# Modulation of an attention and expert block: two thirds summed on VectorE, two gates moved, table loads moved

## Chip, cores and metric

One core of a Trainium2 chip. The metric is the device time of one execution in microseconds (us). Before the change the median of three runs is 3347.15 us.

## What is computed

One layer over 1024 tokens of width 1024, in float32. Cut to what matters here:

```python
mod = silu(c) @ w_ada + b_ada                       # w_ada: 1024 x 6144
shift1, scale1, gate1, shift2, scale2, gate2 = split(mod, 6)
h = rmsnorm(x, g1) * (1 + scale1) + shift1
qa, ka, va, qb, kb, vb, ga, gb = split(h @ w_in)
y_sb = stick_breaking_attention(qa, ka, va)          # 8 heads, strictly causal
y_sw = sliding_window_sink_attention(qb, kb, vb)     # 8 heads, softmax with a sink
x = x + gate1 * ((sigmoid(ga) * (y_sb @ sb_proj) + sigmoid(gb) * (y_sw @ sw_proj)) @ w_out)
h2 = rmsnorm(x, g2) * (1 + scale2) + shift2
# per token 8 heads x top 16 of 16384 experts; expert rows of u and v are gathered
x = x + gate2 * sum(softmax(score) * gelu(h2 . u[e]) * v[e])
out = rmsnorm(x, gf)
```

## The kernel before

The 1024 tokens are eight blocks of 128, in groups of 2, 3 and 3 blocks. Each group goes through the mixer: normalisation and transposes (H), values (V), for each of four pairs of heads the q/k product (QK) and the stick-breaking scores (SB), the window projections (SWP) and window attention (SW), the merge of both branches with gates (MG), the output projection (OUT), and the queries and keys of the expert layer (PREP). Beside the mixer of later groups runs the expert stream: for each block 128 tiles. GpSimd gathers a tile of 128 expert rows of 8 KB (`uv`, line 651) into one of ten ring slots, VectorE takes dot products (line 1597), ScalarE GELU and a diagonal of weights (lines 1270, 1276), TensorE adds up (line 1036), and that frees the slots. No gather can start before the first queries and keys of block 0 are done.

**Order.** Each engine's program is a set of Python generators merged by `interleave`: each yields a key and the smallest key goes next. The order is fixed when the kernel is built, and every engine executes its own list strictly in order, waits included. The keys come from `Plan`, called as `at(stage, group, item, later)`; `later` is added to the key. For group 0 the plan puts H at -208.35, V at -201.14 and -197.45, QK of the four pairs at -192.77, -182.08, -171.40 and -160.72, the first SB step of a pair 4.2 and the second 6.05 behind its QK, SWP at -150.03, SW at -135.40 and MG at -118.66. SyncE issues all transfers but the gathers and five small constants, in one queue.

**Modulation.** `w_ada` is read as 12 column groups of 512, in three thirds of four (`r` = 0, 1, 2), 8.4 MB each. A third fills `wada`, 16384 floats per partition at the start of the ring, in four transfers: two halves of the contraction times two pairs of column groups. TensorE multiplies with `cb`, silu(c) spread over 32 columns: 8 steps `k` times 4 column groups, each group on its own 32 columns of the array, into bank `VACC`. A float32 matmul counts as two instructions in the trace. VectorE adds the bias into `md` and forms 1 + scale times gain. Row 0 (shift 1 and scale 1) is needed for h; rows 1 and 2 (gates, shift 2 and scale 2) are written to `mods_dram` and read back for OUT. In TensorE's order third 1 stands ahead of pair 0, third 2 ahead of pair 1. `wada` is free for the next third when the matmuls of the last one are done (`ada_mm`). The window weights of group 0 go to `RINGO + 1024 * a`, which is inside `wada`.

**Pairs.** The values are stored to `v_dram` (v_scratch in the trace, line 484) and read back per pair (line 500); TensorE waits for that read (`in_vp`) before a pair's scores (line 850). The q/k product of a pair is line 837. For group 0 a pair has two steps, each with logs on ScalarE, a softplus on VectorE (line 1451), sums (lines 865, 870) and values (line 879) on TensorE. The keys of a pair are stored to `k_dram` (line 507); the next pair's ScalarE copy waits for that.

**Window and merge.** In SW, TensorE makes the scores of a block (line 949), the softmax runs on VectorE and ScalarE, TensorE transposes (line 964) and multiplies with the values (line 976). In MG, each of eight column groups has two gate products (`q` = 0, 1; line 731), and two projections (line 734). ScalarE's `Tables.use` issues a table load (line 106) where the next function is in another table than the last.

## Time and profile before

| | |
|---|---|
| median of three runs | 3347.15 us (3343.45 to 3355.85) |
| profiled execution | 3351.51 us, span from first to last instruction 3349.7 us |
| TensorE busy | 2180.0 us (65%) |
| VectorE busy | 2033.7 us (61%) |
| ScalarE busy | 1149.4 us (34%) |
| GpSimd busy | 1113.3 us (33%) |
| moved by DMA | 1267.98 MB, mean 379 GB/s; gathers 1074.03 MB |
| mean granted TensorE clock | 0.798 of full |

The shares are means over a run whose beginning differs from the rest, so they say little about a change in the beginning. The page also cuts the span into 40 slices; read there how busy the DMA engines are, slice by slice. The trace's times are from the start of the span.

### The profile page before, as it was taken

Reading aid. Unit: us, or ns where it says so; the run is one execution under the profiler, and the core shown is the slowest. Engines: PE = TensorE matmul, PEld = TensorE weight load, DVE = VectorE, ACT = ScalarE, POOL = GpSimd, SP = SyncE. Lnnn points to the kernel's source line nnn. Section 1 sums busy time; section 2 is a strip of 40 time slices with the busy share of each in tenths; the row PEclk is TensorE's granted clock in tenths of the full one; section 3 lists DMA queues with packets and bytes.
Section 4 is the critical chain, followed back from the end, with each engine's and each line's share of the span. In section 5 each row is a group of like instructions: output and inputs, shape, how many; then the busy total and the mean of one; then the engine's idle time right before and its main releaser. Section 6 shows DMA issues by size and latency. Waiting matters only on the chain.

```text
span 3349.7 us, 35574 instructions
## 1 busy us (share of the span) xinstructions
PE 2180.0 (65%) x11116; PEld 980.9 (29%) x11116; DVE 2033.7 (61%) x4779; ACT 1149.4 (34%) x3644; POOL 1113.3 (33%) x1033
## 2 busy tenths in 40 slices
PE   5878768877987776777775888577433443344333
PEld 2566633343533332323333333233100000010000
DVE  1022457776656566777667666756666666666754
ACT  1210246733223233676634222222322232222221
POOL 0000124332433333433343333343444444434442
PEclk8989989888998888888897998788765665666565
DMA  9524789989999999999999999999999999999997
GB/s 355 203 87 149 288 345 358 396 360 355 408 416 416 420 406 416 376 415 403 394 408 368 420 419 418 397 417 420 417 421 415 419 408 421 418 416 403 422 421 328
DMA packets 198911, 1267.98 MB, mean 379 GB/s; under 512 B 21609, under 2 KB 35977, under 8 KB 54977
## 3 DMA queue, kind: packets, MB, share of 16 engines
q0 software_dynamic: 147616, 1074.03, 77.9%
q1 hardware_dynamic: 51104, 191.67, 14.9%
q8 instruction: 88, 1.44, 0.2%
q14 instruction: 103, 0.84, 0.1%
HBM read 1244.36 MB, written 21.25 MB: 378 GB/s over the span
## 4 chain that ended last, share of the span: by engine, by line
DMA 38%; PE 35%; issue 10%; ACT 9%; DVE 4%; POOL 1%; SPq 1%; another core or an unknown queue 0%; POOLq 0%; DVEq 0%; ACTq 0%
DMA arena<-in_uv,idx_r 30%; PE pb L1036 12%; PE pb L731 5%; PE pb L816 4%; ACT dg L1276 3%; PE pb L734 2%; DMA arena<-in_w_ada 2%; PE pb L751 2%; DMA arena<-in_w_q 2%; ACT L106 2%; PE pb L1022 2%; PE pb L837 1%; POOL arena L651 1%; DMA v_scratch<-arena 1%; DVE arena L1597 1%
## 5 line engine op out<-in xcount | busy, mean ns | idle before, releaser
L651 POOL DMA_INDIRECT arena<-in_uv,idx_r x1024 | 1110.2, 1084 | 2208.1 <-PE pb L1036 1597.0
L1597 DVE CUSTOM_DVE_ANT_0 arena<-arena 128x1024 f32<-128x1024 f32 x1024 | 1251.6, 1223 | 774.7 <-DMA arena<-in_uv,idx_r 730.9
L1036 PE MATMUL pb<-arena,dg 128*32 128x512 f32 x4096 | 726.1, 845 | 814.6 <-ACT dg L1276 761.2
L1036 PEld LDWEIGHTS pb<-arena,dg 128*32 128x32 f32 x4096 | 132.8, 136 | 1280.2 <-ACT dg L1276 930.1
L1270 ACT ACTIVATE gl<-dots 128x4 f32<-128x4 f32 x256 | 52.9, 207 | 1015.0 <-DVE dots L1597 1002.2
L816 PE MATMUL pb<-arena 128*128 128x384 f32 (+1 forms) x768 | 254.2, 486 | 27.7 <-issue 19.8
L106 ACT ACT_TABLE_LOAD x171 | 219.4, 1283 | 107.9 <-DVE dots L1597 58.8
L1276 ACT ACTIVATE dg<-ig,gl 128x32 f32<-128x32 f32 x1024 | 246.6, 312 | 8.5 <-ACT gl L1270 0.3
L1265 ACT ACTIVATE ig<-istack,gate_r 128x32 f32<-128x32 f32 x1024 | 243.3, 311 | 0.0
L731 PE MATMUL pb<-arena 128*128 128x384 f32 (+1 forms) x768 | 235.4, 459 | 2.4 <-ACT arena L1123 2.4
L816 PEld LDWEIGHTS pb<-arena 128*128 128x128 f32 x768 | 152.2, 205 | 136.5 <-issue 78.5
L731 PEld LDWEIGHTS pb<-arena 128*128 128x128 f32 x768 | 143.6, 191 | 95.8 <-issue 29.1
L751 PE MATMUL pb<-arena 128*128 128x512 f32 x256 | 118.8, 621 | 15.7 <-DVE arena L1438 8.5
L837 PE MATMUL pb<-arena 128*128 128x384 f32 (+1 forms) x384 | 117.8, 460 | 0.0
L734 PE MATMUL pb<-arena 128*128 128x384 f32 (+1 forms) x384 | 117.4, 457 | 0.0
L1451 DVE SCALAR_TENSOR_TENSOR arena<-pb,arena 128x384 f32<-128x384 f32 (+2 forms) x120 | 51.6, 471 | 105.3 <-ACT arena L1205 103.6
L865 PE MATMUL pb<-arena,tri 128*128 128x384 f32 (+2 forms) x240 | 93.2, 482 | 15.4 <-DVE arena L1451 13.8
L1254 ACT ACTIVATE arena<-pb 128x256 f32<-128x256 f32 x112 | 42.9, 383 | 168.1 <-PE pb L1022 156.5
L1022 PE MATMUL pb<-arena,ident 128*32 128x256 f32 x896 | 78.5, 425 | 27.5 <-ACT arena L1254 20.8
L879 PE MATMUL pb<-arena 128*64 128x384 f32 (+2 forms) x240 | 65.1, 491 | 38.4 <-ACT arena L1213 34.4
L837 PEld LDWEIGHTS pb<-arena 128*128 128x128 f32 x384 | 71.7, 192 | 49.7 <-issue 18.3
L850 PE MATMUL pb<-arena 64*128 64x384 f32 (+2 forms) x240 | 57.1, 558 | 43.7 <-DMA arena<-k_scratch 32.0
(157 smaller groups left out, 2217.7 us busy)
## 6 DMA issues: line engine op xcount, KB each, us to landing
arena<-in_w_ada SPq DMA_DIRECT2D x12, 2048.0 KB, 17.8
arena<-in_w_mg SPq DMA_DIRECT2D x24, 1024.0 KB, 5.0
arena<-in_w_q SPq DMA_DIRECT2D x24, 1024.0 KB
arena<-in_uv,idx_r POOLq DMA_INDIRECT x1024
arena<-in_w_qk SPq DMA_DIRECT2D x12, 1024.0 KB, 16.3
arena<-in_w_mg SPq DMA_DIRECT2D x24, 512.0 KB, 5.9
arena<-in_x SPq DMA_DIRECT2D x16, 512.0 KB, 16.4
arena<-in_w_out SPq DMA_DIRECT2D x4, 2048.0 KB, 12.0
```

Source lines behind the costliest of these rows:

```text
L106: self.act.add_instruction(mybir.InstLoadActFuncSet(name=self.nc.get_next_instruction_name(), act_func_set_id=table, engine=mybir.EngineTy ...
L651: pool.indirect_dma_start(ring[:, i % RING, :], None, uv, bass.IndirectOffsetOnAxis(ap=idx_r[:, b % 2, 4 * n + c:4 * n + c + 1], axis=0)). ...
L731: m = pe.matmul(bank, gates[:, q * KT + k, :], hT[:, k, 0:T], start=(k == 0), stop=(k == KT - 1))
L734: m = pe.matmul(bank, projections[:, (q - 2) * 4 + k, :], y[:, k, 0:T], start=(k == 0), stop=(k == 3))
L751: m = pe.matmul(pb[:, BGB + 2 * (j % 2) + i, :], merged[:, k, j * P:(j + 1) * P], f(out_home(g, k) + i * HALF, HALF), start=(k == 0), stop ...
L816: m = pe.matmul(pb[:, BGB + p, 0:T], wq[:, p * KT + k, :], h2T[:, k, 0:T], start=(k == 0), stop=(k == KT - 1))
L837: m = pe.matmul(pb[:, BGB + i, 0:T], wqk[:, i * KT + k, :], hT[:, k, 0:T], start=(k == 0), stop=(k == KT - 1))
L1022: x_ = pe.matmul(pb[32 * q:32 * q + 32, MISC, 256:512], selector(c), h2cur[:, 256 * i:256 * i + 256], start=True, stop=True)
L1036: m = pe.matmul(pb[32 * c:32 * c + 32, VACC + i, :], dg[:, STEP * n // 4 % 2, c, :], ring[:, (STEP * g + c - first) % RING, D + i * HALF:D ...
L1265: op = act.activation(ig[:, half, first + c], istack[:], ACT.Copy, scale=gate_r[:, b % 2, STEP * n + c:STEP * n + c + 1])
L1276: op = act.activation(dg[:, half, first + c], ig[:, half, first + c], ACT.Copy, scale=gl[:, a + c:a + c + 1])
L1597: dve.tensor_tensor_reduce(u, h2rep[:, slot(b, c), :], u, 1.0, 0.0, ALU.mult, ALU.add, dots[:, i % 8:i % 8 + 1]).then_inc(dots_done, 1)
```

## The change

- Third 0 is loaded in quarters of the contraction (two steps `k`, all four column groups), ahead of the biases and gains; TensorE waits quarter by quarter.
- Thirds 1 and 2 are loaded in quarters too, but VectorE sums them: 16 instructions a third, over 2 column groups of 512, each multiplying the weights with silu(c) of its partition and adding to `wsum`. TensorE then adds over partitions with four matmuls of `negones`, and VectorE subtracts the result from the bias. A quarter of third 2 is loaded when the four sums that read its place are done.
- TensorE's product of third 1 now stands ahead of pair 1, that of third 2 ahead of SWP.
- The window weights of group 0 move out of `wada`; these, the table of distances (`alibi`), the merge and the output weights are issued at other places of SyncE's order.
- The two gate products of the first column group of MG in group 0 are made inside SW, into the two accumulator banks.
- In eight places a table load is issued ahead of the semaphore wait and not behind it.

```diff
@@ -251,6 +251,7 @@
         wada = rows(RINGO, 4, 4096)
+        wsum = [rows(YF + 2048 * r, 4, HALF) for r in range(2)]
         md = rows(MD, 3, HALF)
@@ -288,7 +289,9 @@
-            return RINGO + 1024 * a if g == 0 else (X0, X0 + 1024, W0 + 2048, W0 + 6144, B0 + 1536, W0)[a]
+            if g == 0:
+                return (X0, X0 + 1024, RINGO + 18432, W0 + 6144, RINGO + 16384, RINGO + 17408)[a]
+            return (X0, X0 + 1024, W0 + 2048, W0 + 6144, B0 + 1536, W0)[a]
@@ -376,36 +379,40 @@
                     sp.dma_start(small[:, 0:KT], c8).then_inc(in_c, 16)
+                    ada(0, 0)
+                    ada(0, 1)
+                    for j in range(SIZE[0]):
+                        sp.dma_start(xt[:, j, :], x[j * P:(j + 1) * P, :]).then_inc(in_x[j], 16)
+                    ada(0, 2)
+                    ada(0, 3)
                     for c in range(4):
...
                         sp.dma_start(gg[32 * c:32 * c + 32, :], g[(c % 2) * HALF:(c % 2 + 1) * HALF].partition_broadcast(32)).then_inc(in_g, 16)
-                    for k in range(2):
-                        for c in range(2):
-                            ada(0, k, c)
-                        if k == 0:
-                            for j in range(SIZE[0]):
-                                sp.dma_start(xt[:, j, :], x[j * P:(j + 1) * P, :]).then_inc(in_x[j], 16)
                     for i in range(2):
                         value_weights(i)
-                    for p in range(3):
+                    sp.dma_start(f(qk_home(0, 0), 2048), w_qk[0]).then_inc(in_wqk[0], 16)
+
+                def ada(r, i):
+                    sp.dma_start(wada[:, :, 1024 * i:1024 * (i + 1)],
+                                 w_ada[4 * r:4 * r + 4, :, 2 * i:2 * i + 2, :].rearrange("c p k n -> p c (k n)")).then_inc(in_ada[i], 16)
+
+                def mods():
+                    yield at("H", 0, 0, 1)
+                    sp.wait_ge(ada_mm, 1)
+                    for i in range(4):
+                        ada(1, i)
+                    for p in range(1, 3):
                         sp.dma_start(f(qk_home(0, p), 2048), w_qk[p]).then_inc(in_wqk[p], 16)
                     sp.dma_start(sink_row[:], sinks.partition_broadcast(P)).then_inc(in_sink, 16)
-
-                def ada(r, k, c):
-                    sp.dma_start(wada[:, 2 * c:2 * c + 2, 2048 * k:2048 * (k + 1)],
-                                 w_ada[4 * r + 2 * c:4 * r + 2 * c + 2, :, 4 * k:4 * (k + 1), :].rearrange("c p k n -> p c (k n)")).then_inc(in_ada[2 * k + c], 16)
-
-                def mods():
+                    for i in range(4):
+                        yield at("QK", 0, 0, i)
+                        sp.wait_ge(ada_sums, 4 * (i + 1))
+                        ada(2, i)
                     for r in range(1, 3):
-                        yield at("H", 0, 0, 1) if r == 1 else at("QK", 0, 0, 0.6)
-                        sp.wait_ge(ada_mm, r)
-                        for k in range(2):
-                            for c in range(2):
-                                ada(r, k, c)
-                        yield at("QK", 0, r - 1, 0.5)
+                        yield at("QK", 0, 1, 0.5) if r == 1 else at("SWP", 0, 0, 1)
                         sp.wait_ge(md_done, r + 1)
@@ -418,24 +425,29 @@
                     sp.dma_start(f(qk_home(0, 3), 2048), w_qk[3]).then_inc(in_wqk[3], 16)
-                    yield at("QK", 0, 2, -1)
+                    window_weights(0, 3, 1)
+                    yield at("QK", 0, 1, 0.2)
+                    sp.wait_ge(qk_mm, 2)
+                    window_weights(0, 0, 2)
+                    yield at("QK", 0, 2, 0.2)
+                    sp.wait_ge(qk_mm, 4)
+                    window_weights(0, 4, 1)
+                    window_weights(0, 5, 1)
+                    yield at("QK", 0, 3, 0.2)
+                    sp.wait_ge(qk_mm, 6)
+                    window_weights(0, 2, 1)
+                    yield at("SWP", 0, 0, 0.5)
                     sp.wait_ge(ada_mm, 3)
-                    window_weights(0, 0, 2)
-                    window_weights(0, 3, 1)
-                    window_weights(0, 4, 1)
-                    window_weights(0, 2, 1)
-                    window_weights(0, 5, 1)
-                    sp.wait_ge(qk_mm, 2)
-                    sp.dma_start(alibi, consts[:, 2 * P + TOPK + 32:2 * P + TOPK + 32 + TABLE]).then_inc(in_alibi, 16)
                     merge_weights(0, 0)
                     merge_weights(0, 1)
-                    yield at("QK", 0, 3)
-                    sp.wait_ge(qk_mm, 6)
                     out_weights(0, 0, 4)
-                    out_weights(0, 4, 4)
+                    yield at("SWP", 0, 2, 1)
+                    sp.wait_ge(sw_mm, 2)
+                    sp.dma_start(alibi, consts[:, 2 * P + TOPK + 32:2 * P + TOPK + 32 + TABLE]).then_inc(in_alibi, 16)
                     yield at("SW", 0, 0)
...
                     merge_weights(0, 2)
+                    out_weights(0, 4, 4)
                     for ft in range(3, KT):
@@ -655,18 +667,20 @@
                     for r in range(3):
-                        yield at("H", 0, 0, -2) if r == 0 else at("QK", 0, r - 1, -0.01)
+                        yield at("H", 0, 0, -2) if r == 0 else at("QK", 0, 1, -0.01) if r == 1 else at("SWP", 0, 0, -0.01)
                         if r == 0:
                             pe.wait_ge(c_wide, 1)
+                            for k in range(KT):
+                                if k % 2 == 0:
+                                    pe.wait_ge(in_ada[k // 2], 16)
+                                for c in range(4):
+                                    m = pe.matmul(pb[32 * c:32 * c + 32, VACC, :], cb[:, k, :], wada[:, c, k * HALF:(k + 1) * HALF],
+                                                  start=(k == 0), stop=(k == KT - 1))
                         else:
+                            pe.wait_ge(ada_sums, 16 * r)
                             pe.wait_ge(md_done, r)
-                        for k in range(KT):
-                            if k % 4 == 0:
-                                pe.wait_ge(in_ada[k // 2], 16 * (r + 1))
-                                pe.wait_ge(in_ada[k // 2 + 1], 16 * (r + 1))
                             for c in range(4):
-                                m = pe.matmul(pb[32 * c:32 * c + 32, VACC, :], cb[:, k, :], wada[:, c, k * HALF:(k + 1) * HALF],
-                                              start=(k == 0), stop=(k == KT - 1))
+                                m = pe.matmul(pb[32 * c:32 * c + 32, VACC, :], negones[:, 0:32], wsum[r - 1][:, c, :], start=True, stop=True)
                         m.then_inc(ada_mm, 1)
@@ -715,9 +729,10 @@
                             pe.wait_ge(ysw_done, FIRST[g + 1])
-                        pe.wait_ge(in_wmg[mg_turn(g, ft)[0]], mg_turn(g, ft)[1])
+                        if n:
+                            pe.wait_ge(in_wmg[mg_turn(g, ft)[0]], mg_turn(g, ft)[1])
                         gates, projections = rows(mg_home(g, ft)[0], 2 * KT, P), rows(mg_home(g, ft)[1], KT, P)
-                        for q in range(4):
+                        for q in range(2 if n == 0 else 0, 4):
                             o = 4 * ft + q
@@ -897,6 +912,16 @@
                     values(len(steps) - 1)
+
+                def first_gate(q):
+
+                    if q == 0:
+                        pe.wait_ge(in_wmg[mg_turn(0, 0)[0]], mg_turn(0, 0)[1])
+                        pe.wait_ge(md_done, 3)
+                    gates = rows(mg_home(0, 0)[0], 2 * KT, P)
+                    for k in range(KT):
+                        m = pe.matmul(pb[:, VACC + q, 0:SIZE[0] * P], gates[:, q * KT + k, :], hT[:, k, 0:SIZE[0] * P], start=(k == 0), stop=(k == KT - 1))
+                    m.then_inc(mg_mm, 1)
@@ -983,6 +1008,8 @@
                             scores(j + 1)
+                        if g == 0:
+                            first_gate(j)
                         yield at("SW", g, j, 5)
@@ -1046,8 +1073,8 @@
                     yield -2000
+                    table.use(GELU)
                     act.wait_ge(in_c, 16)
-                    table.use(GELU)
                     act.activation(small[:, 8:16], small[:, 0:8], ACT.Tanh, scale=0.5).then_inc(c_tanh, 1)
@@ -1100,8 +1127,8 @@
                         off = CHUNK if b == 0 else 0
+                        table.use(EXP_LN)
                         act.wait_ge(peaked, b + 1)
-                        table.use(EXP_LN)
                         for h in range(SW_HEADS):
@@ -1129,20 +1156,20 @@
                             yield at("MG", g, ft, part(g, 3.8 + 3.7 * q))
+                            if table.now == EXP_LN or table.now == SQRT:
+                                table.use(GELU)
                             act.wait_ge(mg_mm, 4 * n + q + 1)
...
                                 act.wait_ge(mg_done, n - 1)
-                            if table.now == EXP_LN or table.now == SQRT:
-                                table.use(GELU)
-                            act.activation(sg[:, 2 * (ft % 2) + q, 0:T], pb[:, AVB + (4 * ft + q) % 5, 0:T], ACT.Tanh, scale=0.5).then_inc(mg_th, 1)
+                            act.activation(sg[:, 2 * (ft % 2) + q, 0:T], pb[:, VACC + q if n == 0 else AVB + (4 * ft + q) % 5, 0:T], ACT.Tanh, scale=0.5).then_inc(mg_th, 1)
                     for j in range(GB):
...
                         yield at("OUT", g, j, 12.5)
+                        table.use(SQRT)
                         act.wait_ge(o_rinv, b + 1)
-                        table.use(SQRT)
                         act.activation(stats[:, 40 + j:41 + j], stats[:, 36 + j:37 + j], ACT.Sqrt).then_inc(o_rstd, 1)
@@ -1229,8 +1256,8 @@
                             yield topk_at(b, m) + topk_span(b, m) - 1
+                            table.use(EXP_LN)
                             act.wait_ge(picked, n + 1)
-                            table.use(EXP_LN)
                             act.activation(best[:], best[:], ACT.Exp).then_inc(picked_exp, 1)
@@ -1265,8 +1292,8 @@
                             yield STEP * (g + 1) + 0.5
+                            table.use(GELU)
                             act.wait_ge(dots_done, STEP * (g + 1))
-                            table.use(GELU)
                             act.activation(gl[:, a:a + STEP], dots[:, a:a + STEP], ACT.Gelu).then_inc(gelu_done, 1)
@@ -1282,8 +1309,8 @@
                         yield TILES * (b + 1) + 11.5
+                        table.use(SQRT)
                         act.wait_ge(fin_rinv, b + 1)
-                        table.use(SQRT)
                         act.activation(stats[:, 50:51], stats[:, 49:50], ACT.Sqrt).then_inc(fin_rstd, 1)
@@ -1306,12 +1333,27 @@
                     for r in range(3):
-                        yield at("H", 0, 0, -1.5) if r == 0 else at("QK", 0, r - 1, 0.1)
+                        if r:
+                            for n in range(16):
+                                yield at("V", 0, 0, 2 + 0.9 * n) if r == 1 else at("QK", 0, 1 + n // 6, 0.2 + 1.1 * (n % 6))
+                                k, c = n // 2, 2 * (n % 2)
+                                if n % 4 == 0:
+                                    dve.wait_ge(in_ada[n // 4], 16 * (r + 1))
+                                w, total = wada[:, c:c + 2, k * HALF:(k + 1) * HALF], wsum[r - 1][:, c:c + 2, :]
+                                if k == 0:
+                                    dve.tensor_scalar(total, w, cb[:, k, 0:1], None, ALU.mult).then_inc(ada_sums, 1)
+                                else:
+                                    dve.wait_ge(ada_sums, 16 * (r - 1) + n - 1)
+                                    dve.scalar_tensor_tensor(out=total, in0=w, scalar=cb[:, k, 0:1], in1=total, op0=ALU.mult, op1=ALU.add).then_inc(ada_sums, 1)
+                        yield at("H", 0, 0, -1.5) if r == 0 else at("QK", 0, 1, 0.1) if r == 1 else at("SWP", 0, 0, 0.2)
                         if r == 0:
...
                         dve.wait_ge(ada_mm, r + 1)
-                        link(dve.tensor_tensor(md[:, r, :], pb[:, VACC, :], brow[:, r, :], ALU.add))
+                        if r:
+                            link(dve.tensor_tensor(md[:, r, :], brow[:, r, :], pb[:, VACC, :], ALU.subtract))
+                        else:
+                            link(dve.tensor_tensor(md[:, r, :], pb[:, VACC, :], brow[:, r, :], ALU.add))
                         if r == 0:
```

## Rows read from the trace of the kernel before

**Rows 1.** Busy time, granted clock, DMA share and GB/s of two stretches of the whole run.
```profile
150.00:200.00 50.00, 33.42 (x191) 28.56 (x192) 14.03 (x29) 10.98 (x44) 0.00 (x0) 0.78 0.10 37
...
900.00:1200.00 300.00, 235.97 (x1032) 108.67 (x1020) 175.54 (x393) 83.55 (x273) 105.90 (x96) 0.87 1.01 418
```

**Rows 2.** Chain of waits in the first 120 us: start, length, what.
```profile
7.39 24.29 DMA arena<-in_w_ada
...
31.82 5.28 PE pb L668 x32
...
38.57 26.77 DMA arena<-in_w_ada
...
74.70 22.19 DMA arena<-in_w_ada
...
118.38 12.03 DMA arena<-v_scratch
```

**Rows 3.** Timeline of TensorE and SyncE: start, length, engine, line, operation, idle before.
```profile
42.83 16.91 PE L706 MATMUL pb<-arena 128*128 128x512 f32 x32 [3.43 <-DVE arena L1338]
...
69.20 0.34 SPq L500 DMA_DIRECT2D arena<-v_scratch  x1
...
70.73 7.17 PE L837 MATMUL pb<-arena 128*128 128x256 f32 x32
...
78.38 0.49 PE L850 MATMUL pb<-arena 64*128 64x128 f32 x4 [0.47 <-ACT arena L1182]
...
87.56 3.64 PE L668 MATMUL pb<-arena,cb 128*32 128x512 f32 x32
...
102.02 7.17 PE L837 MATMUL pb<-arena 128*128 128x256 f32 x32
...
138.25 7.17 PE L837 MATMUL pb<-arena 128*128 128x256 f32 x32
...
152.97 14.08 PE L914 MATMUL pb<-arena 128*128 128x256 f32 x64
```

**Rows 4.** Fine windows of the DMA engines: 2 KB, 8 KB and 4 KB rows, and the queue running dry.
```profile
5.00:6.00 1.00, 0.00 (x0) 0.00 (x0) 0.00 (x0) 0.00 (x0) 0.00 (x0) 1.00 1.06 231
...
12.00:14.00 2.00, 0.00 (x0) 0.00 (x0) 0.00 (x0) 0.00 (x0) 0.00 (x0) 1.00 1.02 426
...
21.50:22.00 0.50, 0.50 (x8) 0.14 (x4) 0.00 (x0) 0.38 (x3) 0.00 (x0) 1.00 1.05 442
...
67.00:68.00 1.00, 1.00 (x12) 0.36 (x7) 0.00 (x0) 0.00 (x0) 0.00 (x0) 0.50 0.25 81
```

**Rows 5.** VectorE: the three-operand instruction by form, and one softplus in the timeline.
```profile
L1434 DVE SCALAR_TENSOR_TENSOR arena<-arena,stats 128x1024 f32<-128x1024 f32 x2 | 2.6, 1284 | 1.8 <-ACT stats L1146 1.8
...
82.38 0.76 DVE L1451 SCALAR_TENSOR_TENSOR arena<-pb,arena 128x256 f32<-128x256 f32 x2 [0.90 <-ACT arena L1205]
```

**Rows 6.** Timeline of TensorE from the window softmax to the merge.
```profile
178.25 2.77 PE L949 MATMUL pb<-arena 64*128 64x192 f32 x16 [2.53 <-DVE arena L1370]
...
187.49 1.97 PE L964 MATMUL pb<-ident,arena 128*128 128x128 f32 x8 [6.48 <-DVE arena L1387]
...
198.53 3.67 PE L964 MATMUL pb<-ident,arena 128*128 128x128 f32 x16 [6.53 <-DVE arena L1387]
...
205.69 7.17 PE L731 MATMUL pb<-arena 128*128 128x256 f32 x32 [0.69 <-ACT arena L1123]
...
317.47 1.04 PE L744 MATMUL pb<-ident,arena 128*128 128x128 f32 x8
```

**Rows 7.** Timeline of GpSimd: the first gather.
```profile
377.95 1.00 POOL L651 DMA_INDIRECT arena<-in_uv,idx_r  x1 [373.78 <-ACT idx_r L1240]
```

**Rows 8.** Table loads: all of them, their longest cause of idle, and one in the timeline.
```profile
L106 ACT ACT_TABLE_LOAD  x171: 1283/1283/1283, 2.4 to 3343.8; - x171
...
  DVE dots L1597: 58.8, 25
...
371.61 1.28 ACT L106 ACT_TABLE_LOAD   x1
```

4 lines of the change are left out of this document (2 added, 2 removed).

## The prediction

> **What bounds the kernel now.** I read first the page's line of DMA share over forty slices and then two coarse windows [rows 1]. In the window from 900 to 1200 us the DMA engines are busy all the time (share 1.01, 418 GB/s): the gathers of expert rows, 1,074 of 1,268 MB, flow from the first gather to the end of the run. In the window from 150 to 200 us they are nearly idle (share 0.10). The first gather is issued at 377.95 us [rows 7], because it needs the first queries of group 0, and these need the whole mixer of group 0. So the run is an opening of 378 us, and then a stream whose length is bytes over bandwidth. A microsecond taken out of the opening should come off the end nearly whole; one taken out of the stream mostly should not.
>
> Next the chain of waits in the opening [rows 2]. It goes through the three loads of the modulation's weights: TensorE waits for the first third until 31.8, computes until 37.1, and then two more thirds (8.4 MB each) are fetched into the same buffer and multiplied. After that the chain follows TensorE through pairs, window attention, merge and output, with one DMA piece more: 12.03 us for a 0.13 MB read of v_scratch from 118.38. That row matters. The read was queued behind some 7 MB of weights issued from 110 us on, and 7 MB at the 426 GB/s of [rows 4] is 16.5 us: it came out when they had. SyncE's transfers are served in the order of issue, a small one after the large ones ahead of it.
>
> **The head.** The same bytes have to land for the first modulation row: 8.4 MB of weights, 1.05 MB of x, and the 1.05 MB of biases and gains, which are now issued behind them. The biases go in 2 KB rows at 231 GB/s, the weights in 8 KB rows at 426 [rows 4]. Nothing is gained in DMA time by the order. What is gained is the matmul tail: before, half of the third (5.28 us, [rows 2]) stood behind the last landing; now a quarter (about 3.4 us at the low clock) does, and it runs while the biases still come in. The first row is ready near 32 and the values start near 37.6, not 42.83 [rows 3], about 5 us early. They take 16.91 us and the first q/k product 7.17 [rows 3], so pair 0 could score near 62.5. The quarters are 4 KB rows instead of 8 KB ones; x is in 4 KB rows too and ran at 442 GB/s [rows 4], so I price that at nothing. The Trainium skill, "DMA: Bandwidth & Descriptors", section "Why small descriptors are slow (HBM only)", puts the loss at about three cycles per packet, which matters only for rows far below 2 KB; by it the biases too would run at nearly full speed and be in 2 us earlier, but the trace has them at 231 GB/s.
>
> **What is late next.** Pair 0's scores wait for its values, which go through v_scratch: two stores, then a read that waits for both. From the keys of the plan SyncE's new order is: second third (four quarters), q/k weights 1 and 2, sinks, store of block 0, first quarter of the last third (waits for four sums), q/k weights 3 and one head of window weights, store of block 1, read. Count the bytes from about 30.8, when the head's 10.7 MB are in: value and q/k weights 3.1, second third 8.4, q/k weights 2.1, stores 0.5, quarter 2.1, q/k and window weights 1.6: 17.9 MB, at 422 GB/s 42.5 us, so the last store leaves at 73.3. Before, the queue ran dry between 67 and 68 [rows 4] and the read was issued at 69.20 [rows 3]: 1.9 us for the receipt. With that and 2 us for the read, pair 0 scores at 77.5. Before it scored at 78.38 [rows 3]. The 5 us of the head and the 11 us of the second third's matmuls between values and pair 0 (59.7 to 70.73, [rows 3]) end in this wait, and leave 0.9.
>
> **The sums.** Each third becomes 16 VectorE instructions of 128x1024. The trace has this form with three operands at 1,284 ns [rows 5]; the first of a third has two operands, and I take 1,284 for it too (the bounds are 0.6 and 1.3, it hardly matters). That is 20.5 us a third, about the 20 us in which it lands. Second third: quarters land near 44, 49, 54 and 59, and the values' copy stands behind seven sums, done near 53.5, when the values are finished only at 54.5: hidden. Sums 13 to 16 stand around pair 0's softplus. Two stand between the first and the second softplus, where VectorE had 0.90 us of idle time [rows 5]: 2.57 - 0.90 = 1.7 us on the path. In pairs 1 and 2 one sum stands there: 0.4 us each. The others lie beside q/k products of 7.17 us and cost nothing; with that cover gone, 5 of them would cost 6.4 us a pair. TensorE meets pair 0 after some 15 us of idleness, so at the low clock: I add 0.8 us, from the doubling of short matmuls seen in [rows 6] (1.97 us for eight transposes against 1.04), bounds 0 and 2.
>
> The 128 matmul passes of the last two thirds go; four matmuls against a column of minus ones replace each third, no more than one step of eight in the old loop, 0.9 us at full clock (3.64 us for four steps, [rows 3]). The stall of the last third goes as well: 87.56 to 102.02 in [rows 3]. After pair 0: 77.5 + 9.2 (78.38 to 87.56) + 1.7 + 0.8 = 89.2, product 0.9, pair 1 16.3 (102.02 to 118.3) + 0.4, pair 2 at pair 3's length of 14.7 (138.25 to 152.97, [rows 3]) + 0.4, since the window, merge and output weights that stood ahead of the 12.03 us read [rows 2] are now issued later, pair 3 14.7, product 0.9: window projections at 137.5 and not at 152.97, **-15.5**. The store of k of pair 0 and the read for pair 1 are issued behind three quarters, which are in by 92; pair 1 needs them at 97. The table of distances is now loaded behind 5.2 MB from 137 on and is in by 152, needed at 159: hidden, but with 7 us to spare.
>
> **Gates in the softmax's waits.** Two gate products leave the merge: **-7.1** (of the 7.17 at 205.69, [rows 6]). They go where TensorE sat idle 6.48 and 6.53 us [rows 6]. Each is 3.5 us at full clock, 6.9 at half. The first starts right behind 2.8 us of scores at the low clock. If the granted clock rises during it, as it does part way through the values, it fits; if not, it overruns by 0.4. With TensorE kept at work, the transposes and products of block 0 run at full clock: 1.97 to 1.04, and about the same again in the values. The second block's transposes (3.67) may or may not. **-2.5**, bounds 0 and -3.6. First gather: 377.95 - 25.1 = 352.9.
>
> **Table loads.** 171 loads of 1,283 ns [rows 8]. One that is moved ahead of its wait saves at most the idle time in front of it and at most its own length; added up by that rule over all 44 loads with idle time, 47 us, most of it before the GELU (25 loads, 58.8 us idle, [rows 8]). But from 850 us on DMA is saturated, and between 400 and 850 only about 8 us of such loads lie. The load before the exponential of the first block had no idle time (371.61). At the very end the last square root's load gains 0.4. I take **-2.4**, bounds -0.4 and -10. The Trainium skill, "ScalarE: Activation LUTs", section "What ACT_TABLE_LOAD costs", adds a drain and gets 2.66 us per switch; by it this term would be about twice as large. In the trace the exponential follows 0.01 us behind its load, so no drain is seen.
>
> **Sum.** -15.5 - 2.5 - 7.1 - 2.4 = -27.5 us. On the profiled execution (3351.51 us) that gives 3324.0; the median of the runs is 4.4 us lower, so 3319.6, say 3320. A measurement of this kernel can tell about 0.5%, 17 us, from no change.
>
> **Rivals.** (B) The small transfers do not wait behind the large ones, and pair 0 scores near 63: 14 us more, 3306. Against it stands the 12.03 us read. 0.10. (C) 4 KB rows run slower. Between 231 GB/s at 2 KB and 426 at 8 KB, a fixed cost per row gives 331 at 4 KB: over the 18.9 MB of quarters ahead of the read 12 us, and the gain falls to 15: 3332. For it speaks only the interpolation, against it the x row. 0.08. (D) The earlier start does not carry through: groups 1 and 2 or the stream meet a wait tied to something else, and half is lost: 3333. Against it: every later stage is released by the one before, and DMA has no idle time to absorb. 0.10. (E) Slower: VectorE becomes the bound. All 32 sums and the softplus of four pairs stand in one order; at d us each the projections start near 44 + 32 d + 30. At 3.0 us that eats the gain; from 3.4 us on the kernel is slower by over 0.5%, 3365. The measured form speaks against it. 0.04. The forecast holds 0.68, with a range of its own of 3311 to 3329. Range of all: 3306 to 3334. Faster 0.78, same 0.18, slower 0.04.
>
> **What would show it.** Pair 0's first scores (64x128, line of the scores) between 76 and 80, released by the read of v_scratch; if near 63, B. The 32 sums at 1.2 to 1.3 us. q/k of pair 1 near 90; window projections near 137; no idle of 6.5 us in front of the softmax's transposes; first gather near 353. If the first gather is there and the end has not moved by as much, D. The prediction is wrong above all if the order of SyncE's queue is not what I read from the keys, or if a sum stands in front of something that I count as covered.

## The result

The changed kernel runs in 3323.57 us (median of 4, 3318.67 to 3324.24), the kernel before beside it in 3347.68 (median of 4): ratio 0.9922, 95% interval 0.9903 to 0.9941, 24 us less. Run again beside other versions, the same kernel had 0.9903 (0.9879 to 0.9926). The forecast was 3320, 27.5 us less. The profiled execution has a span of 3321.8 us against 3349.7.

The timeline of TensorE and SyncE after the change, in the stretch of [rows 3]:

```profile
40.40 15.36 PE L720 MATMUL pb<-arena 128*128 128x512 f32 x32 [3.43 <-DVE arena L1380]
56.63 7.14 PE L852 MATMUL pb<-arena 128*128 128x256 f32 x32 [0.88 <-DVE arena L1387]
80.11 0.80 PE L865 MATMUL pb<-arena 64*128 64x128 f32 x4 [16.34 <-DMA arena<-v_scratch]
...
90.22 1.42 PE L683 MATMUL pb<-arena,negones 128*32 128x512 f32 x8
91.57 7.17 PE L852 MATMUL pb<-arena 128*128 128x256 f32 x32
...
138.08 14.08 PE L939 MATMUL pb<-arena 128*128 128x256 f32 x64
...
77.64 0.33 SPq L512 DMA_DIRECT2D arena<-v_scratch  x1
```

The values start at 40.40 and not at 42.83, the first q/k product is done at 63.8, and then TensorE stands idle until 80.11, 16.34 us, for the read of v_scratch that SyncE issued at 77.64. This row is the whole of the change's middle: the time freed ahead of pair 0 ended in a wait for 0.13 MB. The read itself took 2.34 us; what took long was the store of 0.26 MB ahead of it, which left only when some 4 MB of weights had gone out before it (windows of DMA from 64.85 to 77.64 add up to 4.5 MB). The window projections start at 138.08, before at 152.97: 14.9 us early. The chain of waits says the same in two rows, the store that had to come out of the queue and the read behind it:

```profile
64.85 12.78 DMA v_scratch<-arena
...
77.64 2.34 DMA arena<-v_scratch
```

DMA, in the view of fine windows (the last two columns are the busy share and GB/s):

```profile
12.00:14.00 2.00, 2.00 (x12) 0.22 (x4) 0.00 (x0) 0.00 (x0) 0.00 (x0) 1.00 1.04 414
45.00:50.00 5.00, 5.00 (x13) 2.15 (x12) 2.92 (x4) 0.60 (x1) 0.00 (x0) 1.00 1.03 411
76.00:77.00 1.00, 0.00 (x0) 0.00 (x0) 0.00 (x0) 0.00 (x0) 0.00 (x0) 0.50 0.28 88
```

With the weights in 4 KB rows the saturated engines move 414 and 411 GB/s, where 8 KB rows gave 426 [rows 4]. The queue runs dry in the microsecond from 76 (share 0.28), nine later than in [rows 4], and then the read goes out.

VectorE's 32 sums by form; the first is the form of [rows 5]:

```profile
L1347 DVE SCALAR_TENSOR_TENSOR arena<-arena,cb 128x1024 f32<-128x1024 f32 x28 | 34.3, 1276 | 1.3 <-DMA arena<-in_w_ada 1.3
...
L1344 DVE TENSOR_SCALAR arena<-arena,cb 128x1024 f32<-128x1024 f32 x4 | 2.8, 745 | 6.8 <-DMA arena<-in_w_ada 6.8
```

They take 1,276 ns with three operands and 745 with two; the idle time in front of them, 8.1 us for all 32, ends with the weights' landing.

From the window softmax to the merge, where [rows 6] has the kernel before (L923 is a gate product, L749 the first projections of the merge, L746 the second column group's gates):

```profile
166.21 5.32 PE L923 MATMUL pb<-arena 128*128 128x256 f32 x16
172.76 1.09 PE L989 MATMUL pb<-ident,arena 128*128 128x128 f32 x8 [1.23 <-DVE arena L1429]
...
175.44 3.72 PE L923 MATMUL pb<-arena 128*128 128x256 f32 x16
182.03 2.65 PE L989 MATMUL pb<-ident,arena 128*128 128x128 f32 x16 [2.87 <-DVE arena L1429]
185.51 3.68 PE L1001 MATMUL pb<-arena 128*64 128x128 f32 x32 [0.83 <-ACT arena L1146]
189.88 5.43 PE L749 MATMUL pb<-arena 128*128 128x256 f32 x16 [0.69 <-ACT arena L1150]
195.15 7.07 PE L746 MATMUL pb<-arena 128*128 128x256 f32 x32
```

Both gate products lie in the waits: 6.48 and 6.53 us of idle time before the transposes have become 1.23 and 2.87. But behind the second gap transposes, values and projections are slow. The granted clock (third figure from the end, 0.50 is 1.2 GHz) shows it:

```profile
179.00:181.00 2.00, 0.16 (x1) 0.00 (x0) 1.15 (x3) 0.75 (x5) 0.00 (x0) 1.00 0.00 0
183.00:185.00 2.00, 1.68 (x10) 1.28 (x7) 0.97 (x2) 0.88 (x2) 0.00 (x0) 0.54 0.00 0
187.00:189.00 2.00, 2.00 (x22) 1.79 (x18) 0.00 (x0) 0.00 (x0) 0.00 (x0) 0.50 0.00 0
```

The first gather and the table loads, next to [rows 7] and [rows 8] (for the gathers count, length in ns, first and last start; for the loads busy time, length of one in ns, and the idle time before them with its longest cause):

```profile
L663 POOL DMA_INDIRECT arena<-in_uv,idx_r x1024: 932/938/1990, 357.8 to 3294.5; - x171
```

```profile
L106 ACT ACT_TABLE_LOAD x171 | 219.4, 1283 | 3.7 <-PEq L1714 0.7
```

The first gather comes at 357.83, 20.1 us early, the last at 3294.5 and not 3321.1, 26.6 us early. The loads' idle time, 107.9 us over all causes before, is down to 3.7. Whether the further 6.5 us come from that was the first question.

### The profile page after: what moved, and what is told of

It is laid out like the page before. It is cut to its first block, busy times and chain, and to the rows that moved or that the text cites. A ratio compares the mean times of both kernels' runs of the same rounds, so it can differ in the third digit from the quotient of the medians.

```text
span 3321.8 us, 35385 instructions
## 1 busy us (share of the span) xinstructions
PE 2152.0 (65%) x11004; PEld 975.3 (29%) x11004; DVE 2068.2 (62%) x4811; ACT 1143.7 (34%) x3644; POOL 1133.2 (34%) x1033
## 4 chain that ended last, share of the span: by engine, by line
DMA 38%; PE 34%; issue 10%; ACT 9%; DVE 4%; another core or an unknown queue 2%; POOL 1%; SPq 1%; POOLq 0%; DVEq 0%; ACTq 0%
DMA arena<-in_uv,idx_r 30%; PE pb L1063 12%; PE pb L746 5%; PE pb L831 3%; ACT dg L1303 3%; PE pb L749 3%; PE pb L766 2%; ACT L106 2%; DMA arena<-in_w_q 2%; DMA v_scratch<-arena 2%; PE pb L852 2%; PE pb L1049 1%; POOL arena L663 1%; DMA arena<-in_w_ada 1%
## 5 line engine op out<-in xcount | busy, mean ns | idle before, releaser
L663 POOL DMA_INDIRECT arena<-in_uv,idx_r x1024 | 1130.1, 1104 | 2161.4 <-PE pb L1063 1571.8
L1063 PE MATMUL pb<-arena,dg 128*32 128x512 f32 x4096 | 706.4, 824 | 804.5 <-ACT dg L1303 724.7
L746 PE MATMUL pb<-arena 128*128 128x384 f32 (+1 forms) x736 | 227.5, 461 | 1.0 <-ACT arena L1150 1.0
L746 PEld LDWEIGHTS pb<-arena 128*128 128x128 f32 x736 | 137.2, 191 | 91.5 <-issue 27.6
L766 PE MATMUL pb<-arena 128*128 128x512 f32 x256 | 117.9, 617 | 18.9 <-DVE arena L1480 10.6
L749 PE MATMUL pb<-arena 128*128 128x384 f32 (+1 forms) x384 | 119.5, 463 | 0.7 <-ACT arena L1150 0.7
## 6 DMA issues: line engine op xcount, KB each, us to landing
arena<-in_w_out SPq DMA_DIRECT2D x4, 2048.0 KB, 11.6
```

The source lines that it names most:

```text
L663: pool.indirect_dma_start(ring[:, i % RING, :], None, uv, bass.IndirectOffsetOnAxis(ap=idx_r[:, b % 2, 4 * n + c:4 * n + c + 1], axis=0)). ...
L746: m = pe.matmul(bank, gates[:, q * KT + k, :], hT[:, k, 0:T], start=(k == 0), stop=(k == KT - 1))
L749: m = pe.matmul(bank, projections[:, (q - 2) * 4 + k, :], y[:, k, 0:T], start=(k == 0), stop=(k == 3))
L766: m = pe.matmul(pb[:, BGB + 2 * (j % 2) + i, :], merged[:, k, j * P:(j + 1) * P], f(out_home(g, k) + i * HALF, HALF), start=(k == 0), stop ...
L1063: m = pe.matmul(pb[32 * c:32 * c + 32, VACC + i, :], dg[:, STEP * n // 4 % 2, c, :], ring[:, (STEP * g + c - first) % RING, D + i * HALF:D ...
```

## Experiments

In each, "first gather" is the first start of line 651 (663 or 664 after the change), and the stream is the time from it to the last one.

**The changed kernel again.**

> The changed kernel once more, as the yardstick for the runs beside it. Both theories: about 24 us under the kernel before (0.9922 was measured), first gather near 358 us.

3317.63 us, ratio 0.9903. Its first gather is at 355.2, 2.6 us before that of the first profile, with the same program. The difference lies in one place:

```profile
173.03 1.45 PE L989 MATMUL pb<-ident,arena 128*128 128x128 f32 x8 [2.70 <-DVE arena L1429]
...
176.95 5.43 PE L923 MATMUL pb<-arena 128*128 128x256 f32 x16
183.53 1.97 PE L989 MATMUL pb<-ident,arena 128*128 128x128 f32 x16 [1.15 <-DVE arena L1429]
...
188.98 3.72 PE L749 MATMUL pb<-arena 128*128 128x256 f32 x16 [0.69 <-ACT arena L1150]
192.54 7.07 PE L746 MATMUL pb<-arena 128*128 128x256 f32 x32
```

Here the first gate ran faster (3.86 us and not 5.32), the gap behind it was 2.70 instead of 1.23, and the clock fell there (granted 0.81 from 173 to 174, then 0.50). The second gate then took 5.43 us, so the gap behind it was only 1.15, and the clock was up from there: 9.0 us from the transposes (183.53) to the second column group (192.54), against 13.1 (182.03 to 195.15). Its stream is 2944.2 us long (355.2 to 3299.4), that of the first execution 2936.7. With its loads ahead of their waits too, this execution took 7.5 us longer behind the first gather than the first one did.

**Table loads back behind their waits**, in the changed kernel.

```diff
-                            table.use(GELU)
                             act.wait_ge(dots_done, STEP * (g + 1))
+                            table.use(GELU)
```

and likewise in the other seven places.

> The changed kernel with all eight table loads back behind their waits. The first gather came 20.1 us earlier, but the span was 27.9 us shorter and the medians 24.1: something saves 4 to 8 us after the first gather. Theory H (the table loads save it, idle time before them fell from 107.9 to 3.7 us): first gather as in the changed kernel within 0.5 us, end 4 to 8 us later, ratio to before 0.9935 to 0.9945. Rival R (the stream just varies from run to run by some us): end the same within 2 us, ratio near 0.992.

3320.11 us, ratio 0.9915 (0.9894 to 0.9936), 2.5 us over the changed kernel run beside it and 3.5 below its first runs: well inside the intervals. First gather 355.7, last 3290.8:

```profile
  DVE dots L1639: 58.1, 25
```

The idle time is back, 58.1 us before the GELU's loads alone, and the stream is 2935.1 us, the shorter one. H's rise of 4 to 8 us is not there, neither in the median nor in the stream. The run speaks for R: the stream scatters from one execution to the next, here by more than the 2 us that R allowed.

**Only the table loads**, in the kernel before.

> The kernel before with nothing but the eight table loads ahead of their waits. Theory R (they are worth nothing that shows: off the path, or on it only where DMA is saturated): ratio 0.999 to 1.001, first gather within 0.5 us of 377.95. My forecast's term: -2.4 us, 0.9993. Rival H (they are what the stream won in the changed kernel): -5 to -8 us, 0.9976 to 0.9985.

3348.63 against 3349.69 us, ratio 0.9996 (0.9984 to 1.0008). Of H, 0.9976 to 0.9985, only the upper end lies inside the interval; the run above speaks against it as well. My term of 2.4 us is inside, and so is nothing. The stream was 2935.0 us (382.2 to 3317.2), the kernel before had 2943.1 (378.0 to 3321.1). Over all thirteen profiles it lies between 2932 and 2944, whatever the kernel. So the further 6.5 us need no other cause than this scatter: the profile of the kernel before had one of the long streams.

R missed in one point: it put the first gather within 0.5 us of 377.95, and it came at 382.2. The rows show why:

```profile
202.80 3.68 PE L976 MATMUL pb<-arena 128*64 128x128 f32 x32 [0.83 <-ACT arena L1119]
207.17 9.02 PE L731 MATMUL pb<-arena 128*128 128x256 f32 x32 [0.69 <-ACT arena L1123]
```

The same two groups took 1.97 us (at 203.03) and 7.17 us [rows 6] in the profile before; here the granted clock was 0.50 from 196 to 210, where it was 1.00 from 204 on before. From the window projections to the second column group this execution took 65.8 us (153.73 to 219.48) and the other 63.2; 0.8 us of the 4.3 were lost before that stretch and 0.9 behind it. One execution can't tell whether the moved loads have a part in where the clock falls. The kernel before has this scatter in its opening too: its first gather lay at 378.0 and 382.2, and that of the changed kernel at 357.8 and 355.2.

**The gate products back in the merge.**

```diff
                         if j + 1 < GB:
                             scores(j + 1)
-                        if g == 0:
-                            first_gate(j)
...
-                        for q in range(2 if n == 0 else 0, 4):
+                        for q in range(4):
```

> The changed kernel without the two gate products inside the softmax: all 16 products of the merge stay in the merge. Theory: from the first window scores to the second column group of the merge the changed kernel takes 35.5 us and the kernel before 41.6, so this one takes 41.6 and its first gather comes 5 to 6 us after that of the changed kernel, near 363.5; ratio near 0.9940. Rival (the gates were worth the 7.1 us that I forecast, and something else ate 2 of them): 365 us and 0.9945.

3327.20 us, ratio 0.9938 (0.9918 to 0.9958). First gather 363.7: 5.9 us after the first profile of the changed kernel, 8.5 after the second. The gates are worth 5.9 or 8.5 us of the opening, according to where the clock falls. This is the theory's 363.5 and not the rival's 365.

**Real work in the gap.** The first projection of the first column group (4 steps, 8 passes) goes behind the second gate, into bank MISC.

```diff
+                    if q == 1:
+                        projections = rows(mg_home(0, 0)[1], KT, P)
+                        for k in range(4):
+                            m = pe.matmul(pb[:, MISC, 0:SIZE[0] * P], projections[:, k, :], ysb[:, k, 0:SIZE[0] * P], start=(k == 0), stop=(k == 3))
+                        m.then_inc(mg_mm, 1)
 # merge, column group 0: q starts at 3 instead of 2, and VectorE takes this product from MISC
```

> The changed kernel, and behind the second gate product also the first projection of the first column group (8 passes, 1.73 us), in the gap before the second block's transposes, into another bank. Theory C (what the gates lost against my 7.1 us is TensorE's clock, which falls in the 2.9 us gap in some executions, and then makes transposes, values and projections take 12 us instead of 7): the granted clock stays at full speed through the gap; from the second block's transposes to the merge's second column group 7.5 to 8 us (9.0 in one execution, 13.1 in the other); first gather 350.5 to 353.5. Rival W (it is only 1.7 us of work moved): first gather 353.5 to 356.

```profile
183.39 1.96 PE L994 MATMUL pb<-ident,arena 128*128 128x128 f32 x16 [1.14 <-DVE arena L1434]
...
190.67 7.07 PE L746 MATMUL pb<-arena 128*128 128x256 f32 x32
```

```profile
183.00:185.00 2.00, 1.61 (x15) 1.62 (x16) 0.81 (x2) 0.48 (x1) 0.00 (x0) 1.00 0.00 0
187.00:189.00 2.00, 1.31 (x23) 1.07 (x19) 0.00 (x0) 0.81 (x3) 0.00 (x0) 1.00 0.00 0
```

7.3 us from the transposes to the second column group, at full clock throughout, and the first gather at 352.3. That is 5.8 us less than in the first profile, of which 1.7 are the eight passes that have left this stretch. Ratio 0.9904 (0.9887 to 0.992); against 0.9922 and 0.9903 of the changed kernel that is within the noise, so only the trace shows this gain.

**Useless work in the gap.** The second gate's first four steps are computed twice.

```diff
+                    for k in range(4 if q == 1 else 0):
+                        pe.matmul(pb[:, VACC + q, 0:SIZE[0] * P], gates[:, q * KT + k, :], hT[:, k, 0:SIZE[0] * P], start=(k == 0), stop=(k == 3))
```

> The changed kernel with eight passes of useless work ahead of the second gate product (its first four steps are computed twice), nothing moved. Theory C: the gap shrinks from 2.9 to 1.2 us and the clock stays up: the stretch from the second block's transposes to the merge's second column group is 9.0 to 9.5 us, first gather 353.5 to 356, so useless work makes the kernel faster than the execution with the clock lost (357.8). Rival: 357 to 359, the extra passes cost or do nothing.

```profile
182.00 1.97 PE L991 MATMUL pb<-ident,arena 128*128 128x128 f32 x16 [1.14 <-DVE arena L1431]
...
191.01 7.07 PE L746 MATMUL pb<-arena 128*128 128x256 f32 x32
```

9.0 us from the transposes to the second column group, first gather 354.0, ratio 0.9909. Nothing was moved and 1.7 us of work added, and the stretch is 4.1 us shorter than in the first profile and as long as in the second. The first profile is the right partner, since up to the second gate the two executions run alike (the first block's transposes at 172.76 and 172.73, 1.09 us each, both at full clock). What was lost there was lost to the clock: C holds. By itself it is one execution, and the unchanged kernel reached 9.0 us without extra passes too. The other runs without them agree: the stretch took 9.0 us behind gaps of 0.68 (early read), 0.85 (loads behind their waits), 1.15 and 2.15 us (longer sums), and more only behind the two longest, 13.1 us behind 2.87 and 10.6 behind 2.86 (spread). The length of the gap alone does not decide it: in the run with longer sums the first block's gap of 2.19 us was followed by slow values (1.97 us for 1.09), the second block's of 2.15 us was not.

**Sums made longer.**

```diff
+                                link(dve.tensor_scalar(w, w, 1.0, None, ALU.mult))
                                 if k == 0:
```

> The changed kernel with every sum on VectorE made longer: ahead of each of the 32 a multiplication of the same weights by 1.0 in place, 0.75 us and a wait for its end, so some 2.2 us a sum and 30 us more of VectorE work in the opening. Theory (the sums lie beside loads and q/k products; only those between two softplus of a pair are on the path): two sums in pair 0, one each in pairs 1 and 2, and some of the five in front of pair 1's softplus, together 5 to 8 us; window projections 143 to 146. Rival E (VectorE's order is the bound as soon as a sum costs more than its quarter's load): 15 us or more, window projections past 153.

```profile
80.02 0.80 PE L865 MATMUL pb<-arena 64*128 64x128 f32 x4 [9.80 <-DMA arena<-v_scratch]
...
91.58 1.90 PE L683 MATMUL pb<-arena,negones 128*32 128x512 f32 x8
...
142.72 14.08 PE L939 MATMUL pb<-arena 128*128 128x256 f32 x64
```

21.9 us of multiplications and their waits were added, and the window projections came at 142.72 instead of 138.08: 4.6 us, a little under the 5 to 8 of the theory. Pair 0 still scores at 80.0, only the idle time in front of it is 9.80 us and not 16.34: all that VectorE did before is hidden by the wait for the read. This run's rival E, 15 us or more, is out by far. E of the prediction began at 3.0 us a sum; the sums took 1.28, and even here 1.97 with the multiplication, so that price was not tried. Ratio 0.9919 (0.9905 to 0.9934), not to be told from the changed kernel's. Its first gather is at 357.8, where the first profile had it: the 4.6 us were given back, since behind a gap of 2.15 us the clock stayed up, and the second block's transposes to the second column group took 9.0 us and not 13.1.

**The read early.** SyncE's order alone.

```diff
 # mods(): behind the second third
-                    for p in range(1, 3):
-                        sp.dma_start(f(qk_home(0, p), 2048), w_qk[p]).then_inc(in_wqk[p], 16)
-                    sp.dma_start(sink_row[:], sinks.partition_broadcast(P)).then_inc(in_sink, 16)
                     for i in range(4):
-                        yield at("QK", 0, 0, i)
+                        yield at("QK", 0, 0, 0.5 + 0.5 * i) if i < 2 else at("QK", 0, 1, -1.1 + 0.1 * i)
 # first_weights(): the two q/k weights and the sinks at QK 0 + 0.35, q/k weights 3 at QK 1 - 0.7
```

> SyncE's order changed alone: the stores of the values and their read for pair 0 stand directly behind the second third; q/k weights 1 and 2, the sinks, q/k weights 3 and a head of window weights go behind them, and the quarters of the last third between the reads. Theory Q (pair 0 waits for a small read behind 7 MB of weights): its scores move from 80.1 to 65 to 67 us, and the first gather from 357.8 to 342 to 346; ratio 0.9875 to 0.9885. Rival V (the sums on VectorE or the product with minus ones take the place of that wait): scores early, but pair 1 starts no earlier than 85 and the first gather stays above 350; ratio above 0.990.

```profile
65.79 0.49 PE L866 MATMUL pb<-arena 64*128 64x128 f32 x4 [1.74 <-DMA arena<-v_scratch]
...
76.36 7.17 PE L853 MATMUL pb<-arena 128*128 128x256 f32 x32
...
102.43 0.80 PE L866 MATMUL pb<-arena 64*128 64x128 f32 x4 [2.89 <-ACT arena L1210]
...
63.42 0.33 SPq L513 DMA_DIRECT2D arena<-v_scratch  x1
...
85.56 0.35 SPq L520 DMA_DIRECT2D k_scratch<-arena  x1
```

```profile
85.56 16.35 DMA k_scratch<-arena
```

Pair 0 scores at 65.8 and pair 1's q/k product starts at 76.4 instead of 91.6, as Q says; V had it no earlier than 85. Ratio 0.9874 (0.9848 to 0.99); first gather 345.0, at the late end of the range, since a new wait took 3 us and the clock with it: the store of pair 1's k, 16.35 us in a queue of weights again.

**Loads spread over the pairs.**

```diff
 # mods(): the four quarters of the last third (against the run above)
-                        yield at("QK", 0, 0, 0.5 + 0.5 * i) if i < 2 else at("QK", 0, 1, -1.1 + 0.1 * i)
+                        yield at("QK", 0, 0, 0.5) if i == 0 else at("QK", 0, (1, 1, 2)[i - 1], -0.9)
 # first_weights(): q/k weights 2 at QK 1 - 0.95, q/k weights 3 at QK 2 - 0.95,
 # window weights at QK 2 - 0.8 (one head) and QK 3 - 0.9 (the others)
```

> As the run with the early read, but the big loads spread over the pairs: behind pair 0's read q/k weights 1 and the first quarter of the last third; behind pair 1's read q/k weights 2 and two quarters; behind pair 2's read q/k weights 3, the last quarter and a head of window weights; behind pair 3's read the other window weights. Theory Q: the wait for the store of k (16.35 us in the chain of the run before, ahead of pair 2) goes, pair 2 scores near 99 instead of 102.4 and at full clock, window projections near 122 instead of 128.2, first gather 337 to 340. Rival: another small transfer or the sums (their quarter now comes later) hold pair 2 or 3, and the first gather stays at 343 or more.

In the timeline of TensorE, VectorE and SyncE:

```profile
77.17 7.17 PE L852 MATMUL pb<-arena 128*128 128x256 f32 x32
...
89.50 0.71 PE L880 MATMUL pb<-arena,tri 128*128 128x128 f32 x4 [3.13 <-DVE arena L1493]
...
95.94 7.68 PE L852 MATMUL pb<-arena 128*128 128x256 f32 x32
...
87.96 1.28 DVE L1347 SCALAR_TENSOR_TENSOR arena<-arena,cb 128x1024 f32<-128x1024 f32 x1 [5.79 <-DMA arena<-in_w_ada]
...
76.83 0.98 SPq L399 DMA_DIRECT2D arena<-in_w_ada  x2
```

Ratio 0.9868 (0.9852 to 0.9885), but the first gather was at 344.4 and the window projections at 126.9. I had expected 337 to 340 and 122, and the rival won: the store waits no more, but now VectorE stands idle 5.79 us for a quarter of the last third (issued at 76.83 behind pair 1's read), with pair 1's softplus behind that sum in its order. Pair 1 takes 18.8 us for it (77.17 to 95.94). In the softmax, behind a gap of 2.86 us before the second block's transposes, the clock fell here as well (0.50 from 173 to 175) and cost 1.6 us.

**Spread, and the gap filled.** Two edits from above in one kernel: the loads of the spread run and the real work in the gap.

> Both together: spread loads, and the first projection in the gap. If the two are independent: first gather 331 to 335, ratio to before 0.984 to 0.987. If the start carries through to the end as it did before, the end moves as far as the first gather, within 4 us.

3302.93 us, ratio 0.9866 (0.985 to 0.9883). The ratio is in the range, the first gather is not: 340.2 and not 331 to 335, by the same idle time (3.73 us ahead of pair 1's sums on TensorE), which the expectation did not know of. It is 4.2 us before the spread run's, and the last gather 4.6 us (3272.5 and 3277.1); medians 2.2 us apart don't tell the two versions apart. Against the first profile of the changed kernel the first gather moved by 17.6 us and the last by 22.0, 4.4 us apart, just outside the 4 us expected and inside the stream's scatter.

**Two quarters behind pair 0's read.** On top of the version before.

```diff
-                        yield at("QK", 0, 0, 0.5) if i == 0 else at("QK", 0, (1, 1, 2)[i - 1], -0.9)
+                        yield at("QK", 0, 0, 0.5) if i < 2 else at("QK", 0, i - 1, -0.9)
```

> As the run with spread loads and the gap filled, but the second quarter of the last third is issued with the first, behind pair 0's read; one quarter each stays behind pair 1's and pair 2's read. In the run before VectorE stood 3.1 to 3.7 us in front of pair 1's softplus, because the fifth sum of the last third is ahead of it in its order and needs the second quarter, which had been issued only behind pair 1's read. Theory: that wait goes, pair 1's scores to pair 2's q/k product shrink from 11.5 to under 9.5 us, window projections 121.5 to 123, first gather 335.5 to 338. Rival: the store of k of pair 0, now behind one quarter more, holds pair 1 instead and nothing is gained (340 or later).

```profile
77.38 7.17 PE L852 MATMUL pb<-arena 128*128 128x256 f32 x32
...
92.09 7.17 PE L852 MATMUL pb<-arena 128*128 128x256 f32 x32
...
123.86 14.08 PE L944 MATMUL pb<-arena 128*128 128x256 f32 x64
```

The wait of VectorE is gone: pair 1 takes 14.7 us (77.38 to 92.09), against 18.8 in the spread run. Window projections 123.9, first gather 338.3, both just outside what I expected: pair 0 had the low clock (granted 0.50 from 68 to 76) and took 11.5 us to pair 1's q/k product (65.88 to 77.38), where the run before took 8.9 (65.66 to 74.58). 3304.91 us, ratio 0.9868 (0.9851 to 0.9886), not to be told from the run before. Both are some 0.4 to 0.6% under the changed kernel and are the versions that I would keep.

## Why the prediction was right

**Opening and stream.** Right. Over all thirteen profiles the first gather moved by 44 us, from 382.2 to 338.3, and the stream kept its 2932 to 2944 us: the end moves with the first gather, give or take these 12 us. Rival D fell.

**The head.** Mis-sized. I had 5 us early, and the values came 2.4 early. The slower 4 KB rows explain about a third of the 2.6 us between: 9.4 MB at 410 GB/s are 22.9 us, at 426 22.1. The last quarter's matmuls started at 29.71. Why the last quarter's landing and the gains (VectorE waited for them until 34.84) came still later was not tested. Beyond the bytes counted in the next step it cost nothing here: the DMA engines were busy without a break from 4 to 75 us, and TensorE waited for them anyway.

**What is late next.** The mechanism was right and carries the forecast: I put pair 0's scores at 77.5 by counting bytes in SyncE's queue, they came at 80.1. The 27.3 MB that had to move first, without the 2 KB rows, take 66.4 us at 411 GB/s and 64.7 at 422: 1.7 of the 2.6 us. Rival C was true in kind and wrong in price (3% and not 22%). That the wait was the queue is shown by the early read: with SyncE's order alone changed, pair 0 scored at 65.8. The Trainium skill, "DMA: Bandwidth & Descriptors", section "Queues, rings and completion order", has each DMA engine consume the descriptors of a ring in order; the 12.78 us store and the 16.35 us one agree.

**The sums.** Right in kind: 1,276 ns for three operands, and hidden but for what stands between two softplus. I had 1,284 for the two-operand ones too, which took 745. Pair 0 took 10.1 us and not the 11.7 I summed, pairs 1 and 3 14.7 (I had 16.7 and 14.7), pair 2 16.1 (15.1). Pair 1 of the kernel before, which I had copied, ran partly at the low clock (granted 0.62 from 114 to 118); in the changed kernel the low clock fell on pair 2 (0.50 from 119 to 121). The window projections came at 138.08 against 137.5: +2.6 for the read, -1.6, -2.0 and +1.0 for pairs 0 to 2 and +0.5 for the product. That they cancelled to 0.6 us is luck.

**Gates in the waits.** The step that was most off in the first profile. I had 9.6 us with the clock's gain (-7.1 and -2.5); from the window projections to the second column group the kernel before takes 63.2 us (152.97 to 216.15), the changed one 57.1 or 54.2. So 6.1 or 9.0 (with 65.8 for the kernel before, as in the run with its loads moved, 8.7 or 11.6). I had bounded the second block's transposes from below by no gain, but not seen that the projections of the merge behind them could lose: with the clock lost the first column group's projections took 5.43 us. The experiments with real and with useless work in the gap show the cause.

**Table loads.** -2.4 was forecast. Measured alone: 0.9996, 1.1 us less by the medians, anything from 5.4 us gained to 2.7 lost. That they are off the path or lie where DMA is saturated was argued from the trace; shown is only that 8 us are out.

**Sum.** In place of -15.5, -9.6 and -2.4: -14.9, -6.1 (or -9.0), about 0, and 0.9 us lost between the output projection, which starts 21.0 us early (268.93 for 289.92: 14.9 and 6.1), and the first gather. It lies in the first product of the queries, 9.59 us (from 307.90, line 831) for 8.70 (from 328.90, line 816); the rows around it are alike. There the granted clock was 0.50 until past 312, over 4 us into the product, and in the kernel before it was back at 0.99 after 3 us. First gather -20.1 or -22.8 against the one profile of the kernel before; the medians -24 and -32, with up to 12 us of scatter in the stream and some 4 us in the opening from one execution to another. The forecast of -27.5 lies between the two medians. No run took the -14.9 apart: what the quarters of the head, the moved products and the sums are worth is read from the timeline, and only the wait for the read and the price of the sums were tried by themselves.

## What to carry to other kernels

Count the bytes that stand in a queue ahead of every small transfer on which an engine waits: 0.26 MB behind some 4 MB took 12.8 us, and freeing the engine before it only lengthens the wait. Work taken off one engine and given to another is paid where the other's fixed order puts it ahead of something on the path, not by its sum: 22 us more of sums moved the window projections by 4.6. And where a gap of 2.9 us was left before short, dependent matmuls, eight useful passes in it made the stretch behind it 5.8 us shorter than where the clock had fallen; look for such passes first. What a profile shows of a few us is one execution: take a second one of the same kernel before explaining it.

## What the runs showed of the hardware

- The clock at one place differs from execution to execution of the same program: behind a gap of 2.87 us, with full clock ahead of it, it stood at half (1.2 GHz, granted 0.54 from 183 to 185, then 0.50); behind 1.15 us it stayed at full (1.00 from 181 to 191), and in the run with longer sums behind 2.15 us too. In the other profile it had fallen one gap earlier and risen again in time. With added useless passes the stretch was 4.1 us shorter than in the execution that lost the clock there.
- Saturated DMA engines moved 406 to 414 GB/s with 4 KB rows of weights (10 to 26 us after the change) and mostly 422 or 426, once 414, with 8 KB rows (10 to 18 and 26 to 36 us before it); I had read 442 from half a microsecond of x.
- Rows of 2 KB, the biases and gains spread to the partitions, ran at 211 to 253 GB/s (28 to 34 us after the change, 205 to 252 from 4 to 8 us before it), with the DMA share at 1.0 or above.
- Issuing DMAs took SyncE longer behind others: the second pair of quarters and the biases took 5.71 and 8.48 us (from 3.67 and 9.42), where the kernel before, which issued the biases first, took 1.84 for them.
